# Four-layer transformer on one Trainium2 core: begun FFN and attention tiles in twos of 512 columns, last two turned back later, last attention step scaled head by head

## The reference, cut to what matters

```python
def swiglu(h, w_in, w_out):
    gu = h @ w_in
    return (jax.nn.silu(gu[..., :D_FF]) * gu[..., D_FF:]) @ w_out
...
def conv_ffn(h, w_up, ffn_conv_w, w_down):
    u = h @ w_up
    a, b = u[..., :D_FF_2], u[..., D_FF_2:]
    a = causal_dwconv(a, ffn_conv_w)
    return (jax.nn.gelu(a.astype(F32), approximate=False) * b.astype(F32)).astype(h.dtype) @ w_down
...
def dilated_mixer(h, w_qkv, w_o, rel_bias):
    b, s_len, _ = h.shape
    qkv = (h @ w_qkv).reshape(b, s_len, DIL_GROUPS, 3, DIL_HEADS, DIL_HEAD_DIM)
...
    alpha = jax.nn.softmax(jnp.stack(lses, axis=0), axis=0)
    o = jnp.sum(alpha[..., None] * jnp.stack(outs, axis=0).astype(jnp.float32), axis=0).astype(h.dtype)
    return o.reshape(b, s_len, DIL_HEADS * DIL_HEAD_DIM) @ w_o
```

## Time and profile before

| | |
|---|---|
| median of 3 runs | 1442.26 us (1441.75 to 1443.47) |
| the profiled execution's own time | 1443.14 us |
| its span, first to last instruction | 1441.3 us |
| PE busy | 1419.8 us (99%) |
| POOL busy | 1058.8 us (73%) |
| ACT busy | 746.8 us (52%) |
| DVE busy | 662.6 us (46%) |
| granted TensorE clock, mean | 0.999 of full speed |

### The profile page before, as it was taken

How to read it: one execution, slowest core, us unless ns; L and a number is a source line. 1 busy time by engine, 2 the same in 40 slices (tenths; PEclk the granted TensorE clock), 3 DMA queues, 4 the chain that set the end, 5 groups by cost and what they waited for, 6 DMA issues and landing times.

```text
span 1441.3 us, 21531 instructions
## 1 busy us (share of the span) xinstructions
PE 1419.8 (99%) x8654; PEld 1255.9 (87%) x8654; DVE 662.6 (46%) x1404; ACT 746.8 (52%) x997; POOL 1058.8 (73%) x262
## 2 busy tenths in 40 slices
PE   7999999999999999999999999999999999999997
PEld 6989888889899899798888889998888899998886
DVE  5646545034343333364540444666650566556614
ACT  6885545344666656565543445544543246344540
POOL 5376988865766666769888668759889677688891
PEclk9999999999999999999999999999999999999999
DMA  6576555555656556455555565355565555365560
GB/s 230 174 279 212 196 179 201 184 183 182 214 172 194 188 173 196 146 203 187 190 190 176 182 252 191 113 192 188 181 219 197 209 200 185 117 217 192 186 223 29
DMA packets 64667, 271.12 MB, mean 188 GB/s; under 512 B 6123, under 2 KB 28833, under 8 KB 37954
## 3 DMA queue, kind: packets, MB, share of 16 engines
q1 hardware_dynamic: 39704, 242.31, 49.3%
q10 hardware_dynamic: 24873, 27.53, 5.7%
HBM read 268.68 MB, written 8.21 MB: 192 GB/s over the span
## 4 chain that ended last, share of the span: by engine, by line
PE 94%; ACT 3%; DVE 2%; DMA 0%; issue 0%; SPq 0%; DVEq 0%; ACTq 0%
PE psum L464 90%; PE psum L656 1%; PE psum L942 1%; PE psum L542 0%; ACT w_hi L1130 0%; ACT prob L1362 0%; DMA h<-x 0%; PE psum L824 0%; PE psum L781 0%; PE psum L1088 0%; DVE xt_both L1703 0%; ACT q_rows L1329 0%; ACT prob L1446 0%; PE psum L1045 0%; ACT prob L1440 0%
## 5 line engine op out<-in xcount | busy, mean ns | idle before, releaser
L456 POOL TENSOR_TENSOR w_lo<-raw,w_hi 128x2048 fp32r<-128x2048 f32 (+2 forms) x248 | 1045.5, 4231 | 343.9 <-ACT w_hi L1130 343.9
L1130 ACT ACTIVATE w_hi<-raw 128x2048 fp32r<-128x2048 f32 (+2 forms) x248 | 432.1, 1753 | 139.5 <-DMA raw<-w_tail 87.3
L464 PE MATMUL psum<-xt_both,w_hi 128*128 128x512 f32 (+1 forms) x1920 | 442.7, 371 | 0.0
L464 PEld LDWEIGHTS psum<-xt_both,w_hi 128*128 128x128 f32 x1920 | 340.3, 189 | 57.1 <-issue 3.6
L464 PE MATMUL psum<-w_hi,xt_both 128*128 128x256 f32 (+3 forms) x1328 | 316.7, 328 | 0.5 <-DVE xt_both L1703 0.5
L464 PE MATMUL psum<-xt_both,w_lo 128*128 128x256 f32 x1728 | 253.5, 283 | 0.0
L464 PEld LDWEIGHTS psum<-w_hi,xt_both 128*128 128x128 f32 x1328 | 229.5, 190 | 15.4 <-issue 0.9
L464 PEld LDWEIGHTS psum<-xt_both,w_lo 128*128 128x128 f32 x1728 | 233.7, 191 | 7.5
L464 PE MATMUL psum<-w_lo,xt_both 128*128 128x256 f32 (+3 forms) x664 | 211.2, 326 | 0.0
L464 PEld LDWEIGHTS psum<-w_lo,xt_both 128*128 128x128 f32 x664 | 126.3, 190 | 7.1
L1218 ACT ACTIVATE lanes<-lanes 128x256 f32<-128x256 f32 x88 | 36.7, 418 | 166.5 <-DVE lanes L1740 107.8
(11 more groups left out here) (216 smaller groups left out, 1401.7 us busy)
## 6 DMA issues: line engine op xcount, KB each, us to landing
raw<-w_tail SPq DMA_DIRECT2D x156, 1024.0 KB, 4.9
raw<-w_dil SPq DMA_DIRECT2D x24, 1024.0 KB, 4.8
raw<-w_mix SPq DMA_DIRECT2D x24, 1024.0 KB, 4.9
raw<-w_dil SPq DMA_DIRECT2D x16, 576.0 KB, 3.7
bias_tiles<-bias_rows ACTq DMA_DIRECT2D x1, 6912.0 KB
gbuf<-gain_rows ACTq DMA_DIRECT2D x12, 512.0 KB, 5.0
dbias<-bias_tiles ACTq DMA_DIRECT2D x16, 384.0 KB, 5.8
raw<-w_dil SPq DMA_DIRECT2D x8, 384.0 KB, 4.6
```

The lines of the kernel that those rows point to most:

```text
L456: nc.gpsimd.tensor_tensor(w_lo[:, s, 0:width], raw[:, s, 0:width], w_hi[:, s, 0:width].bitcast(F32), ALU.subtract).then_inc(lo_split, 1)
L464: return nc.tensor.matmul(dst, lhsT, rhs, start=start, stop=stop)
L1130: nc.scalar.activation(w_hi[:, s, 0:width], raw[:, s, 0:width], ACT.Copy).then_inc(hi_split, 1)
```

## The change

Begun tiles are taken in twos. The weights of two tiles are packed together, so that a chunk holds half of the 1024 features for 512 columns, and a matmul moves 512 columns instead of 256. The first two feed-forward parts begin four tiles instead of three; the dilated attention still begins two, the last two feed-forward parts four. `copy_rows` copies 512 columns at once. The first two's transposes back stand in the middle of the next two's block 1, and the last two's stand after the first seven matmuls of the following normal tile. Some banks are named anew. An activation of one column, `preset`, is put ahead of each feed-forward part's first activation.

In the dilated attention's last step DVE inverts head 0's sums before the last far part of head 1, and ACT scales each head right after its exponentials. ACT's copy of weight chunk `C_WO` + 2 goes ahead of all this, and that of `C_WO` + 3 moves from between the two `d_pcopy` to behind both.

```diff
-ROWS_AT = {T_FFN0: ((3, 4, 7), (5, 6, 0)), T_DIL: ((4, 5), (6, 7)), T_FFN1: ((0, 1, 5), (4, 3, 0)),
-           T_FFN2: ((0, 1, 6, 7), (4, 5, 0, 1)), T_FFN3: ((0, 1, 6, 7), (4, 5, 0, 1))}
...
+ROWS_AT = {T_FFN0: ((3, 4), (5, 6)), T_DIL: ((4,), (6,)), T_FFN1: ((0, 1), (3, 6)),
+           T_FFN2: ((6, 7), (0, 1)), T_FFN3: ((6, 7), (0, 1))}
+TURNED_AT = {t: (1, 3) if t == T_DIL else (2, 3, 0, 1) for t in ROWS_AT}
+TWOS = {t: len(at[0]) for t, at in ROWS_AT.items()}
...
+                def part(k, views, tb, midway=lambda: None):
                     tok = slice(tb * P, (tb + 1) * P)
...
+                    for half, (hi, lo) in enumerate(views):
+                        for j in range(KT // 2):
+                            kt = half * KT // 2 + j
+                            arrive(t, tb, kt)
+                            ins = split_x(psum[:, bank, :], xt_hi[:, kt, tok], xt_lo[:, kt, tok],
+                                          hi[:, j, :], lo[:, j, :], kt == 0, kt == KT - 1)
+                        if tb == 1:
+                            ins.then_inc(chunk_used, 1)
+                        if half == 0:
+                            midway()
...
+                def views_of(k):
+                    for half in range(2):
+                        if k == twos - 1 and half == 1:
+                            turn_block(t, 1)
+                        yield chunk(c + 2 * k + half, BANK)
...
+                for k in range(twos):
+                    part(k, views_of(k), 0)
+                for k in range(twos):
+                    part(k, [chunk(c + 2 * k + half, BANK) for half in range(2)], 1,
+                         (lambda: turn_back(k - 1)) if k > 0 else lambda: None)
+                then(lambda: turn_back(twos - 1))
...
-                copy_rows(t, 0, range(max(held - 2, 0), held))
+                copy_rows(t, 0, range(max(twos - 1, 0), twos))
                 ahead(c + 2, LEAD)
-                copy_rows(t, 1, range(held if t == T_DIL else min(held, 2)))
+                copy_rows(t, 1, range(min(twos, 1)))
...
+                nc.scalar.activation(preset[:, l:l + 1], ident[:, 0:1], func)
...
-                    if u + 2 < BEGUN[T_FFN[l]]:
-                        copy_rows(T_FFN[l], 1, [u + 2])
+                    if u == 0:
+                        copy_rows(T_FFN[l], 1, [1])
...
+            ahead(C_WO[1])
             d_out(last - 1)
-            d_exp(last, 0)
-            ahead(C_WO[1])
-            d_exp(last, 1)
-            d_pscale(last, 0)
-            d_pscale(last, 1)
+            for hh in range(2):
+                d_exp(last, hh)
+                d_pscale(last, hh)
             d_pcopy(last, 0)
+            d_pcopy(last, 1)
             ahead(C_WO[1] + 1)
-            d_pcopy(last, 1)
             ahead(C_WO[1] + 1, LEAD)
             d_out(last)
...
+                        if col == 2 and not ahead:
+                            invert(0)
+                for hh in range(0 if ahead else 1, 2):
+                    invert(hh)
```

More of the change, by code:

```diff
@@ L204, in build @@
         lanes = sb("lanes", [P, 2, LANES, SEQ])
+        preset = sb("preset", [P, 5])
         with ExitStack() as part:
@@ L515, in begin_tiles @@
             def begin_tiles(t, c, then):
-                held = BEGUN[t]
-                def part(k, hi, lo, tb):
+                twos = TWOS[t]
+                def part(k, views, tb, midway=lambda: None):
                     tok = slice(tb * P, (tb + 1) * P)
[L522 to L536, removed]
-                def turn_back(k):
[L538 to L551, removed]
+                    bank = ROWS_AT[t][tb][k]
+                    for half, (hi, lo) in enumerate(views):
[8 more added lines that the diff above has]
+                            midway()
@@ new lines, in part @@
+                    if tb == 0:
+                        ins.then_inc(rows_made, 1)
+                def views_of(k):
[3 more added lines that the diff above has]
+                        yield chunk(c + 2 * k + half, BANK)
+                def turn_back(k):
+                    pe.wait_ge(rows_copied, TB * TWOS_BEFORE[t] + twos + k + 1)
+                    for u in range(2):
+                        for half in range(2):
+                            for tb in range(TB):
+                                at = half * SEQ + tb * P
+                                f = (2 * u + half) * P
+                                ins = nc.tensor.transpose(psum[:, TURNED_AT[t][2 * k + u], at:at + P],
+                                                          first_rows[:, k, tb, f:f + P], ident[:, :])
+                        ins.then_inc(rows_turned, 1)
@@ L976, in d_step, with then @@
                 d_values_sum(pair, par)
-            begin_tiles(T_DIL, C_DIL, lambda: turn_r(3, T_DIL))
-            d_tiles(2, 0)
+            def then(turn_last):
+                turn_r(3, T_DIL)
+                d_tiles(2, 0, turn_last)
+            begin_tiles(T_DIL, C_DIL, then)
             for n in range(3):
@@ L1206, in ffn @@
                 func = ACT.Silu if l < 2 else ACT.Gelu
+                nc.scalar.activation(preset[:, l:l + 1], ident[:, 0:1], func)
                 ahead(C_IN[l], LEAD)
                 held = BEGUN[T_FFN[l]]
+                ahead(C_IN[l] + 1, LEAD)
                 for u in range(FT):
@@ L1962, in d_step @@
                             d_lo(pair - 1)
-                for hh in range(2):
-                    dve.wait_ge(d_exped, 4 * pair + 2 * hh + 2)
-                    v.reciprocal(rinv_q[:, :, hh:hh + 1], rsum_q[:, :, hh:hh + 1]).then_inc(d_inverted, 1)
+                        if col == 2 and not ahead:
+                            invert(0)
+                for hh in range(0 if ahead else 1, 2):
+                    invert(hh)
                 if ahead:
@@ L2145, in paired, with begun @@
             for j in range(n)]
+def begun(w, twos, n, left, right, step=P):
+    out = []
+    for j in range(0, 2 * twos, 2):
+        cols = np.concatenate([np.arange(at + u * step, at + u * step + P) for u in (j, j + 1) for at in (left, right)])
+        out += [tile(w, range(half * KT // 2, (half + 1) * KT // 2), cols) for half in range(2)]
+    return out + paired(w, n, left, right, step)[2 * twos:]
 def by_three(w, cols):
@@ L2174, in pack @@
         vcols = np.concatenate([np.arange(at(g, 2), at(g, 2) + P) for g in range(NG)])
-        steps.append([paired(wd, 1, at(g, 0), at(g, 1))[0] for g in range(NG)] + by_three(wd, vcols))
+        tiles = begun(wd, TWOS[T_DIL] if i == 0 else 0, NG, at(0, 0), at(0, 1), 3 * D)
+        steps.append(tiles + by_three(wd, vcols))
     out["w_dil"] = steps
```

47 lines of the change are left out of this document (26 added, 21 removed).

## The result

The changed kernel takes 1446.42 us (median of 16 runs, 1445.88 to 1447.66), against 1442.97 us (1441.75 to 1445.01, 16 runs) of the kernel before: 3.5 us slower, ratio 1.0022 with a 95% interval of 1.0015 to 1.0030. The forecast was 1439.0, and no case of the prediction held this result's cause.

The account below looks back on a forecast made before the run. PE, busy 1419.8 of 1441.3 us, was taken to bound the kernel. Savings of 2.4 + 0.45 + 1.15 - 1.0 + 0.3 = 3.3 us took the median from 1442.26 to 1439.0, range 1437.2 to 1440.8.

Parts of the forecast that it names:

- These three: Wider copies, `preset` and renamed banks: taken at nothing; uncovered, 0.2 us a copy, at most 0.2 for `preset`, and bank waits.
- The forecast's sign: Whole kernel against the kernel before: faster 0.52, same 0.44, slower 0.04, with the line at 1439.4 us.
- Third and fourth part, 2.4: Last two feed-forward parts, four begun tiles each: wider matmuls save 8 x 0.30 = 2.4 us.
- the choice of the mixer's row: Wide begun matmuls priced at the hybrid mixer's 227.3 ns, saving 12.5 ns per narrow pair; the skill's rule gave 2.5.
- Dilated attention, 0.45: Two begun tiles there save 0.60 us, of which 0.15 goes into PE's wait for DVE before the second transposes.
- First and second part, 1.15 less 1.0: First two feed-forward parts: wider matmuls save 0.58 us each, 1.15 together; a new wait loses 1.0 together.
- The cost of turning early: First two feed-forward parts: PE waits 0.5 us in each for ACT's copy before the last two's transposes, 1.0 lost.
- The attention's last step, 0.3: Dilated attention's end: PE's 2.13 us wait goes, the sum comes 1.4 us earlier, but POOL's late `w_lo` leaves 0.3 gained.
- the upper bound: Attention's last step: 1.4 us gained if POOL has `w_lo` in time for `wo3(0)`; the lower bound was 0.
- late for a chunk in the begun tiles: Rival "further waits", chance 0.22: POOL's fourth chunk or a similar one slips, 0.5 to 2 us go, 1439.5 to 1441.
- The rival that ended slower: Chance 0.04: ACT's row copy waits behind `C_IN` + 5's late transfer in all four feed-forward parts, 6.4 us lost, 1445.4.
- The rival with pace as its matter: Chance 0.06: wide begun matmuls go at 235 ns, no cheaper; the 432 lose 3.3 us and nothing is left, 1442.3.

Follow-up runs that it names:

- the base: The changed kernel with the preset column written into the unused tile `phase`, so without `preset` as a tile of its own: 1440.11 us, ratio 0.9977 to the kernel before.
- the twos alone: The changed kernel with `preset` written into `phase` and the attention's last step as before the change: 1439.99 us, ratio 0.9977 to the kernel before.
- the last experiment: Changed kernel, `preset` in `phase`, first two parts' last two turned behind the whole tile, ACT's copy of `C_WO` + 3 before head 0's exponentials: 1437.47 us, ratio 0.9953.

## Why the prediction was wrong

The step that failed is this one: "`preset` moves no load of an activation table onto the path [...] These three I take at nothing; uncovered they would cost [...] at most 0.2 for the preset itself." The price of the instruction was right: in the first part it takes 0.20 us on ACT, with 5.6 us of idle time behind it. What was not looked at is the tile that it writes to: it shifts `ht_hi` and `ht_lo` by 32 bytes against the weights, and that costs 6.3 us (1446.42 less 1440.11) to 7.2 us (the tile alone in the kernel before), 6.7 in the long pieces of either pair of traces. Nothing else is needed for the miss, since with 256 bytes for the tile the kernel takes 1439.86, and the range was 1437.2 to 1440.8. The forecast's sign failed with that one step.

The other steps can be read off by stage in the trace of the base, where the matmuls that hold `ht` run at the old pace.

*Third and fourth part, 2.4.* From the start of block 0 to the end of the chain's long piece the third part took 185.7 us before and takes 184.6 (943.14 to 1127.70); the fourth gives the same. Together 2.35: right. So is the pace of 227 ns. The fixed cost in the Trainium skill (TensorE: Matmul & The Clock Gate, "Wait — 56ns, not 53.3ns?") would have given almost nothing back; the twos alone gave 3.4 us, so the choice of the mixer's row was right.

*Dilated attention, 0.45.* The piece of 76 matmuls started at 361.70 before and starts at 361.29 in the base, with the second transposes at 335.98 in both: 0.41.

*First and second part, 1.15 less 1.0.* The net of 0.08 for each was right: the second part took 186.71 us before (610.49 to 797.20) and takes 186.63 (610.02 to 796.65). The cost of turning early shows in the chain and the waits of the changed kernel:

```profile
140.46 0.44 DVE rb_ffn L1671
140.92 0.44 DVE lanes L1747
141.38 0.42 ACT lanes L1235
141.80 0.49 ACT t L1214
142.34 1.09 PE psum L552 x8
```

```profile
PE psum L467 <- POOL w_lo L459: 1.3, 1, 1.3
PE psum L954 <- ACT probT L1468: 1.1, 1, 1.1
...
PE psum L552 <- ACT t L1214: 0.6, 2, 0.3
```

PE waits 0.3 us rather than 0.5, but its eight transposes then take 1.09 instead of 0.87, so the sum is 0.5 after all. Turning behind the whole tile took these 0.5 away: the second part is down to 186.12 us (609.56 to 795.68). For both parts that is the 1.0 of the forecast; the median fell by 1.3 (1440.11 to 1438.85).

*The attention's last step, 0.3.* The mechanism was right, the size was not. The chain of the changed kernel has the steps in the order forecast: ACT's scaling, its copy, PE's transposes, the second copy, the weight copy, POOL, and then `wo3(0)` on PE.

```profile
591.41 1.45 ACT prob L1463 x2
592.86 1.02 ACT probT L1468
594.02 1.19 PE psum L954 x9
595.23 1.13 ACT probT L1468
596.36 1.80 ACT w_hi L1145
598.23 4.61 POOL w_lo L459
602.98 8.45 PE psum L467 x36
```

The 2.13 us of the earlier trace rows are gone, and PE waits 1.1 and 1.3 us instead, the second before `wo3(0)`, where I had said "about 1". But in the kernel before with this part alone, the stage from 571.69 to 610.95 lasts 39.26 us, and before it 39.07 (571.42 to 610.49): 0.2 lost instead of 0.3 gained. Counted from the stage's start, `wo3(0)` was forecast at 30.5 us and came at 30.8 (602.51 less 571.69). The working had put the transposes of 1.19 us too short and had left out most of the handovers of 0.02 to 0.14 us between engines. The rest lies behind `wo3(0)`'s start. The medians show no difference (ratio 0.9996). That POOL's lateness was the bound is shown by the last experiment: with the weight copy ahead of the exponentials the stage takes 37.7 us (570.31 to 608.00). That is 1.4 less than in the kernel before, the upper bound that the prediction gave "if POOL is in time".

The stages add up to 2.7 us (2.35 + 0.41 + 0.16 - 0.2), and the spans of the two profiled executions differ by 2.9 (1441.3 and 1438.4). The medians differ by 3.5 (1443.65 and 1440.11). Of the rest some 0.4 us, by the estimate in the last section, may be a fall of the clock that kernels with the old last step of the attention have.

The rivals: POOL was never late for a chunk in the begun tiles, ACT's copies came in time in the last two parts, and wide matmuls were cheaper than two narrow ones. The rival that ended slower named 1445.4, close to the result by accident: its mechanism, a late transfer, doesn't appear among the waits. The rival with pace as its matter looked only at the matmuls that the change rewrites.

## What to carry to other kernels

A new tile is a change to every tile that is allocated behind it, also where its instructions are free: round small tiles up to 256 bytes a partition (64 was not enough here), or compare the starting addresses of all matmul operands before and after. Small tiles allocated last would move nothing; that was not run. When PE is busier with fewer matmuls, group them by form and look for a group that the change doesn't touch. A wait that is replaced should be priced with each handover between engines, since a few tenths of a microsecond decide whether anything is left.

## What the runs showed of the hardware

**Matmuls' pace hangs on how the operands lie to one another.** With all stationary and moving tiles of a stream in phase at 256 bytes, a matmul that moves 512 columns has a pace of some 227 ns here; with stationary tiles out of phase to the moving ones by 32, 64, 96 or 128 bytes it is 4 to 7 ns slower, 2 to 3%, and 256 bytes restore it. One tile out of phase also slows matmuls beside it whose own two tiles are in phase (`ht_hi` with `ht_lo` moved, 394 and 395 ns for 390 and 389). Where all lie together made no difference in the three places tried. The group of 256-column matmuls did not slow (283 ns in phase, 281 and 282 with `xt_both` out of phase). In the whole kernel this was worth 23.5 us, from 1440.1 to 1463.6.

The Trainium skill (TensorE: Matmul & The Clock Gate, "Step-by-step: what each phase is for") says that PE reads the moving operand and the next weights through two independent ports, so that a load steals nothing from the running matmul. By that rule these shifts would cost nothing. The runs disagree by 1.3 to 1.7 us in 258 matmuls, so somewhere the two reads, or a read and what else goes on, meet. Where is open: a clash between the load of the next stationary tile and the running stream would fit that moving `ht_lo` alone slows its neighbours, but on that account only one stream in three meets a load out of phase, 0.6 of the 1.69 us, and 1.32 were measured. Whether phases other than 0, 32, 64, 96 and 128 bytes, or tiles of other types, behave so was not tried.

**After a wait of 2.1 us the clock fell in two traces of three.** Three profiled kernels have the old last step of the attention, and in all three PE stands idle for 2.1 to 2.2 us before head 0's transposes, as in the earlier trace rows: the kernel before, the kernel before with the unused tile, and the twos alone. In the first the granted clock stays at 1.00. In the twos alone PE then ran below full clock. Windows (us, busy time of PE, PEld, DVE, ACT, POOL, granted clock, DMA share, GB/s) of that run:

```profile
592.10:596.07 3.97, 3.97 (x19) 3.36 (x16) 0.00 (x0) 3.20 (x3) 1.45 (x2) 0.57 0.25 105
596.10:602.10 6.00, 6.00 (x54) 4.88 (x53) 0.43 (x1) 5.75 (x5) 6.00 (x2) 1.00 0.00 0
```

A granted clock of 0.57 is for most of the stretch the lower level, 1.2 GHz. The kernel with the unused tile did the same: 0.57 from 594.84 to 598.81, and 1.00 behind it. Its timeline of PE shows the wait, then two matmuls in 1.06 us at the lower level and two in 0.62 at full clock:

```profile
593.88 1.21 PE L943 MATMUL psum<-ident,prob 128*128 128x128 f32 x9 [2.13 <-ACT prob L1447]
...
595.59 1.06 PE L465 MATMUL psum<-w_lo,ot_hi 128*128 128x512 f32 x2
...
599.82 0.62 PE L465 MATMUL psum<-w_hi,ot_lo 128*128 128x512 f32 x2
```

In both the stage took 40.36 us (570.61 to 610.97, and 573.32 to 613.68) instead of 39.07, so one fall costs 1.3 us. The changed kernel has 1.00 behind its shorter waits of 1.1 and 1.3 us.

The mean granted clock of whole runs points the same way. It is below 0.998 in 28 of the 89 runs of the kernel before that were timed beside the experiments, in 3 of 8 of the twos alone and in 3 of 5 of the kernel with the unused tile. In the 129 runs of the kernels with the new last step it never is. So the new step seems to spare the fall, a gain that the stages above leave out; over all runs it would be some 0.4 us (an estimate: 1.3 us in 28 of 89). The mean is a rough sign: the traced run of the twos alone has the fall and a mean of 0.998. That each low mean is this same fall is not shown, since only one run of a kernel has a trace. Nor do the runs show why a wait of this length brings the lower level in one run and not in another.
